# Rotating q and k heads on VectorE alone, scan steps in three operations, and some weight remainders made earlier

## The reference

```python
xn = rmsnorm(x, norm_mix)
u, q, k, v, qi, ki, wi, gl = split(xn @ w_in)
q = rope(rmsnorm(q, q_norm), pos)          # 8 heads of 128
k = rope(rmsnorm(k, k_norm), pos)          # 4 heads of 128
# rope: x1, x2 = halves of a head
#       concatenate([x1*cos - x2*sin, x2*cos + x1*sin])
y_att = attend(q, k, v, qi, ki, wi, pos)   # indexer picks the top keys
# S5: h[t] = a*h[t-1] + (b u)[t], complex, 64 groups x 64 states
y_ssm, h_re, h_im = s5_scan(u, h0, a, b, c, d)
y_ssm = gelu(y_ssm); y_ssm *= sigmoid(y_ssm @ w_glu)
x = x + (gate0 * (y_ssm @ w_br0) + gate1 * (y_att @ w_br1)) @ w_out
x = x + (silu(hn @ w_gate) * (hn @ w_up)) @ w_down   # hn = rmsnorm(x)
```

## Time and profile before

| what | before |
|---|---|
| median of three runs | 3066.21 us |
| profiled execution, its own time | 3065.53 us |
| its span, first to last instruction | 3063.7 us |
| busy: PE, DVE, ACT, POOL | 3006.6, 1956.3, 1240.4, 253.4 us |
| granted TensorE clock, mean over the span | 0.998 |

### The profile page before, as it was taken

One profiled execution on the slowest core, in us unless ns is written; L12 is line 12 of the kernel. 1 busy time (PEld: TensorE's weight loads), 2 busy tenths in 40 slices (PEclk: granted clock), 3 DMA queues, 4 the chain that ended last, 5 costly groups with the idle time before them and its releaser, 6 DMA issues. The chain is left out here.

```text
span 3063.7 us, 58940 instructions
## 1 busy us (share of the span) xinstructions
PE 3006.6 (98%) x23528; PEld 2860.5 (93%) x23528; DVE 1956.3 (64%) x3397; ACT 1240.4 (40%) x1735; POOL 253.4 (8%) x239
## 2 busy tenths in 40 slices
PE   7999999999999999999999999999999999999999
PEld 7988878999999999999989888789999999999999
DVE  7559868577656545565575697785776555456553
ACT  4443333544554333434334422335435453333432
POOL 4320000400000000000043200004000000000000
PEclk9999999999999999999999999999999999999999
DMA  6447434745555655556555573347455556555564
GB/s 249 163 153 196 144 125 137 246 168 177 198 182 181 200 170 178 179 184 206 186 188 167 156 196 127 126 147 244 167 175 199 185 178 201 170 178 182 183 208 134
DMA packets 150194, 546.47 MB, mean 178 GB/s; under 512 B 19825, under 2 KB 25073, under 8 KB 149521
## 3 DMA queue, kind: packets, MB, share of 16 engines
q1 hardware_dynamic: 137296, 507.40, 49.3%
q0 software_dynamic: 12096, 35.67, 4.6%
q10 hardware_dynamic: 640, 1.16, 0.1%
HBM read 536.95 MB, written 7.21 MB: 178 GB/s over the span
## 5 line engine op out<-in xcount | busy, mean ns | idle before, releaser
L1795 DVE TENSOR_TENSOR w_ffn_low<-ring_ffn,w_ffn_high 128x1024 fp32r<-128x1024 f32 (+1 forms) x480 | 638.7, 1331 | 456.9 <-ACT w_ffn_high L1289 456.8
L1289 ACT ACTIVATE w_ffn_high<-ring_ffn 128x1024 fp32r<-128x1024 f32 (+1 forms) x480 | 548.0, 1142 | 641.7 <-PE main L1016 641.5
L1014 PE MATMUL main<-x_ffn_high,w_ffn_high 128*128 128x264 f32 x2816 | 792.5, 281 | 0.0
L1016 PE MATMUL main<-x_ffn_high,w_ffn_low 128*128 128x264 f32 x2816 | 792.1, 281 | 0.0
L1015 PE MATMUL main<-x_ffn_low,w_ffn_high 128*128 128x264 f32 x2816 | 792.1, 281 | 0.0
L1014 PEld LDWEIGHTS main<-x_ffn_high,w_ffn_high 128*128 128x128 f32 x2816 | 527.1, 187 | 0.1
L1015 PEld LDWEIGHTS main<-x_ffn_low,w_ffn_high 128*128 128x128 f32 x2816 | 527.1, 187 | 0.1
L1016 PEld LDWEIGHTS main<-x_ffn_high,w_ffn_low 128*128 128x128 f32 x2816 | 527.1, 187 | 0.0
L1014 PE MATMUL main<-hidden_high,w_ffn_high 128*128 128x264 f32 x1408 | 396.1, 281 | 0.0
L1015 PE MATMUL main<-hidden_low,w_ffn_high 128*128 128x264 f32 x1408 | 396.1, 281 | 0.0
L1016 PE MATMUL main<-hidden_high,w_ffn_low 128*128 128x264 f32 x1408 | 396.1, 281 | 0.0
(11 more groups left out here) (378 smaller groups left out, 4804.0 us busy)
## 6 DMA issues: line engine op xcount, KB each, us to landing
ring_ffn<-in_w_up SPq DMA_DIRECT2D x352, 512.0 KB, 3.3
ring<-in_w_in SPq DMA_DIRECT2D x260, 512.0 KB
ring_ffn<-in_w_down SPq DMA_DIRECT2D x128, 704.0 KB, 4.1
ring<-in_w_br SPq DMA_DIRECT2D x64, 512.0 KB
ring<-in_w_out SPq DMA_DIRECT2D x64, 512.0 KB
w_low<-in_w_in POOLq DMA_DIRECT2D x20, 512.0 KB, 7.0
ring<-in_w_glu SPq DMA_DIRECT2D x16, 512.0 KB
out_x<-x SPq DMA_DIRECT2D x8, 528.0 KB, 5.9
```

The source lines that it names most:

```text
L1014: mm(out, wfh[:, slot, w], high[:, kk, :], start=kk == 0, stop=False)
L1016: m = mm(out, wfl[:, slot, w], high[:, kk, :], start=False, stop=kk == chunks * kts - 1)
L1289: af(wfh[:, s, 0:cols], ring_ffn[:, s, 0:cols], ACT.Copy).then_inc(high_ready, 1)
L1795: tt(wfl[:, s, 0:cols], ring_ffn[:, s, 0:cols], wfh[:, s, 0:cols].bitcast(F32), ALU.subtract).then_inc(low_ready, 1)
```

## The change

Five things change.

1. **Heads are rotated by VectorE alone.** The 12 products with `rot128` and their waits go. VectorE makes the crossed part itself: rows 64 to 127 of the head, times -1 and sin, go to rows 0 to 63 of a buffer, and rows 0 to 63 times sin to rows 64 to 127; then head times cos, and the sum. These 12 x 4 instructions now stand right behind `skip(0)`, beside the second state input, with the lows of units 102 to 105 after every second head. TensorE's pieces of units 106 and 107 become two whole units.
2. **A scan step takes three operations.** One product of 1024 elements makes both parts, with factors from a table that holds, for each tile and each of re and im, the factor of the same part and (negated for im to re) that of the crossed part; then an add of 512 and a crossed add of 512, which reads re and im in the opposite order. Each waits for the one before. The last 15 steps are the same three operations, no longer with two pairs of buffers.
3. **ScalarE makes the tables** (`coefficients`): 8 copies per scan, four of 256 elements and four of 48. For the first scan they stand between the copy of the score and the first state input's copies; for the second behind the copies of v. The scans wait for them.
4. **Lows are made earlier** in the discretization: 13 with 12, 14 and 15 instead of 13 and 14, then 16 before the far powers, 17 and 18 behind them.
5. A semaphore is renamed (`bbt_copied` is now `s5_copied`) and also counts the tables.

```diff
@@ TensorE, after the v transposes
-                    for t in range(12):
-                        pe.wait_ge(qnormed, t + 1)
-                        if t >= 2:
-                            pe.wait_ge(qrot_used, t - 1)
-                        mm(side[t % 2][:, 0:T], rot128, proj[:, K + t, :], start=True, stop=True).then_inc(qrot_ready, 1)
-                        if t % 3 == 1:
-                            w_in_piece(53, t // 3 * 4, 4)
+                    w_in_blocks(53, 1)
@@ ScalarE
+                    def coefficients(half):
+                        tiles = slice(HALF * half, HALF * half + HALF)
+                        for near in (True, False):
+                            table = step_coef[half] if near else far_coef[:]
+                            for kind in range(2):
+                                power = apow[:, kind, :, tiles] if near else far_pow[:, :, kind, tiles]
+                                for c in range(2):
+                                    af(table[:, :, kind, c:ST:2], power, ACT.Copy, scale=-1.0 if kind and c else 1.0).then_inc(s5_copied, 1)
...
+                    act.wait_ge(cneg, 1)
+                    coefficients(0)
                     act.wait_ge(pi_done, 2)
                     bu(0)
...
                         af(vnat[:, b, :], side[2 + b][:, :], ACT.Copy).then_inc(v_copied, 1)
+                    act.wait_ge(units, 106)
+                    coefficients(1)
                     evac_gates(50, 4)
@@ VectorE, discretization
-                    lows_to(12)
+                    lows_to(13)
...
                         if n == 8:
-                            lows_to(14)
+                            lows_to(15)
+                    lows_to(16)
...
-                    lows_to(16)
+                    lows_to(18)
                     dve.wait_ge(c_in, 16)
@@ VectorE, scan
-                            m1, ins = products(pw1, prev, pr, n)
-                            st.mark(ins)
-                            m2, ins = products(pw2, prev, pi, n)
-                            st.link(ins)
-                            st.link(tt(cur, cur, m1, ALU.add))
-                            st.mark(tt(cur[:, :, 0, :], cur[:, :, 0, :], m2[:, :, 1, :], ALU.subtract))
-                            st.link(tt(cur[:, :, 1, :], cur[:, :, 1, :], m2[:, :, 0, :], ALU.add))
+                            m = pw[:, 0:ST * 2 * n].rearrange("p (k m n) -> p k m n", k=2, n=n)
+                            was = prev.rearrange("p s c n -> p (s c) n").unsqueeze(1).to_broadcast([P, 2, ST, n])
+                            st.link(tt(m, was, coef.unsqueeze(3).to_broadcast([P, 2, ST, n]), ALU.mult))
+                            own, crossed = (m[:, kind].rearrange("p (s c) n -> p s c n", c=2) for kind in range(2))
+                            st.link(tt(cur, cur, own, ALU.add))
+                            st.link(tt(cur, cur, crossed[:, :, ::-1, :], ALU.add))
...
                             if j < CH - 1:
-                                m1, ins = products(buf1, last, apow[:, 0, j, tiles], NC - 1)
...
+                                fma(hh[:, :, :, NC * j + 1:NC * j + NC], last, near[:, j], NC - 1)
@@ VectorE, rotation
-                    lows_to(105)
+                    lows_to(101)
+                    dve.wait_ge(qnormed, NHK)
                     for t in range(12):
-                        dve.wait_ge(qrot_ready, t + 1)
+                        tile, buf = proj[:, K + t, :], th[:, t % 2, :]
                         if t >= 2:
                             dve.wait_ge(qroped, t - 1)
-                        rope(proj[:, K + t, :], side[t % 2][:, 0:T], cosq, sinq, th[:, t % 2, :], qrot_used, qroped)
+                        st.mark(stt(buf[0:HD // 2], tile[HD // 2:HD], -1.0, sinq[HD // 2:HD], ALU.mult, ALU.mult))
+                        st.link(tt(buf[HD // 2:HD], tile[0:HD // 2], sinq[0:HD // 2], ALU.mult))
+                        st.link(tt(tile, tile, cosq, ALU.mult))
+                        tt(tile, tile, buf, ALU.add).then_inc(qroped, 1)
+                        if t % 2:
+                            lows_to(min(102 + t // 2, 105))
```

More of the change, by code:

```diff
@@ L142, in build @@
         far = sb("far", [P, 6 * ST])
+        far_coef = sb("far_coef", [P, 3, 2, ST])
         qb = sb("qb", [P, 4, 32])
@@ L279, in build @@
         ktr = cc[:].rearrange("p a b c -> p (a b c)").rearrange("p (b n) -> p b n", b=2)
+        step_coef = [a.rearrange("p (j k m) -> p j k m", j=CH, k=2) for a in (
+            vnat[:].rearrange("p b n -> p (b n)"), bbt[:, 0].rearrange("p f s -> p (f s)"))]
         powers = apow[:].rearrange("p a b c -> p (a b c)")
@@ L312, in build @@
         rows_out = tmp[:, 384:512]
-        pw1, pw2 = tmp[:, 0:512], tmp[:, 512:1024]
+        pw = tmp[:, 0:1024]
         one_hot = rs[:, 1, 0:2 * NHK]
@@ L663, in _ @@
                         if g >= 2:
-                            pe.wait_ge(bbt_copied, g - 1)
+                            pe.wait_ge(s5_copied, g - 1)
                         for j in range(4):
@@ L682, in _ @@
                     pe.wait_ge(proj_copied, 10)
-                    pe.wait_ge(bbt_copied, 3)
+                    pe.wait_ge(s5_copied, 3)
                     for b in range(2):
@@ L689, in _ @@
                     pe.wait_ge(qb_ready, 1)
-                    pe.wait_ge(bbt_copied, 4)
+                    pe.wait_ge(s5_copied, 4)
                     pe.wait_ge(irot_used, 9)
@@ L1573, in scan, with fma @@
                         tiles = slice(HALF * half, HALF * half + HALF)
[L1576 to L1583, removed]
-                            m1, ins = products(pw1, prev, pr, n)
-                            st.mark(ins)
-                            m2, ins = products(pw2, prev, pi, n)
-                            st.link(ins)
-                            st.link(tt(cur, cur, m1, ALU.add))
-                            st.mark(tt(cur[:, :, 0, :], cur[:, :, 0, :], m2[:, :, 1, :], ALU.subtract))
-                            st.link(tt(cur[:, :, 1, :], cur[:, :, 1, :], m2[:, :, 0, :], ALU.add))
-                        a1r, a1i = apow[:, 0, 0, tiles], apow[:, 1, 0, tiles]
+                        dve.wait_ge(s5_copied, 4 + 8 * (half + 1))
+                        def fma(cur, prev, coef, n):
+                            m = pw[:, 0:ST * 2 * n].rearrange("p (k m n) -> p k m n", k=2, n=n)
[4 more added lines that the diff above has]
+                            st.link(tt(cur, cur, crossed[:, :, ::-1, :], ALU.add))
+                        near = step_coef[half]
                         turns = 0
@@ L1607, in scan @@
                         for k in range(4):
                             back, ends = 1 << k, SEQ - NC
-                            pr, pi = (apow[:, c, CH - 1, tiles] if k == 0 else far_pow[:, k - 1, c, tiles] for c in range(2))
                             turn()
-                            fma(hh[:, :, :, ends + back:SEQ], hh[:, :, :, ends:SEQ - back], pr, pi, NC - back)
+                            fma(hh[:, :, :, ends + back:SEQ], hh[:, :, :, ends:SEQ - back],
+                                near[:, CH - 1] if k == 0 else far_coef[:, k - 1], NC - back)
@@ L1613, in scan @@
                         last = hh[:, :, :, SEQ - NC:SEQ - 1]
-                        made = {}
                         for j in range(CH):
                             turn()
-                            buf1, buf2 = pairs[j % 2]
                             if j < CH - 1:
-                                m1, ins = products(buf1, last, apow[:, 0, j, tiles], NC - 1)
-                                made[j] = [m1, st.mark(ins)]
-                            if j >= 1:
-                                cur, (m, n1, w, n2) = hh[:, :, :, NC * (j - 1) + 1:NC * j], made[j - 1]
-                                st.after(n2)
-                                added = st.mark(tt(cur, cur, m, ALU.add))
-                            if j < CH - 1:
-                                if j >= 2:
-                                    st.after(done)
-                                m2, ins = products(buf2, last, apow[:, 1, j, tiles], NC - 1)
-                                made[j] += [m2, st.mark(ins)]
-                            if j >= 1:
-                                st.after(added)
-                                st.mark(tt(cur[:, :, 0, :], cur[:, :, 0, :], w[:, :, 1, :], ALU.subtract))
-                                done = st.mark(tt(cur[:, :, 1, :], cur[:, :, 1, :], w[:, :, 0, :], ALU.add))
```

12 lines of the change are left out of this document (5 added, 7 removed).

## The result

| | before | after |
|---|---|---|
| median of the runs | 3068.84 us (4 runs, 3065.42 to 3075.17) | 3043.06 us (4 runs, 3039.68 to 3045.59) |
| ratio, 95% interval | | 0.9913 [0.9892, 0.9934] |
| span of the profiled execution | 3063.7 us | 3039.8 us |
| busy: PE, DVE, ACT | 3006.6, 1956.3, 1240.4 us | 2994.0, 1965.2, 1247.8 us |

A forecast was written before the change was run, and what follows sets the result against it. TensorE was taken to bound the kernel, with products in a row and few waits. Per layer 7.1 + 1.2 + 2.7 + 1.9 - 1.4 = 11.5 us, twice 23.0, gave 3043 us; range 3032 to 3059.

The forecast's parts named there:

- Rotations: TensorE from the v transposes to the first logits: 16.15 us become about 8.95, so 7.1 us less per layer.
- The cover of 8 us: VectorE's rotated heads are done about 1943, needed from 1950.6 on; gone only at 2.3 us per head.
- The step: A scan step on VectorE takes 2.71 us instead of 2.85; each of the last 15 takes 2.57 instead of 2.33.
- First scan: Beside the bisection: 2.0 us back in the first part, 0.8 lost at the end; 1.2 us less per layer.
- Attention: Beside the second scan: shorter rounds and VectorE entering about 1.1 us ahead cut softmax waits by 2.7 us per layer.
- Low parts: TensorE's waits for lows 13 and 15 go, as these are made earlier: 1.9 us less per layer, bounds 0.5 and 2.4.
- Tables: ScalarE's first eight copies delay the state input's copies, costing 1.4 us per layer; the second eight cost nothing.
- The clock: TensorE's granted clock falls to 1.2 GHz around the picks in layer 1; it can give or take 3 us.
- D: Rival: rotations' gain kept, other waits don't shrink, tables cost 2.6 us; 6 us per layer, 3053 us; 15 in 100.
- A: Rival: links between VectorE instructions are free, last scan steps take about 2.2 us; 3.6 us more gain, 3040; 8 in 100.
- B: Rival: the scan step stays at 2.85 us, last steps 2.71; gain of 2.8 us per layer, 3060; 12 in 100.
- C: Rival: the scan's crossed add pays for stepping backward; at double time 68 us lost in all, 3134; 7 in 100.

The follow-up runs named there:

- e1: The kernel before with only the change's rotations on VectorE; scan and low parts as before, no tables: 3051.06 us, ratio 0.9933 to before.
- e7: The changed kernel with each rotation's two half-height instructions reading the rows they write, so heads aren't rotated properly: 3043.43 us in one run.
- e6: The changed kernel with the crossed add reading re and im in their order, so the scan adds the wrong part: 3042.81 us in one run.
- e5: The changed kernel with each scan's last 15 steps as four instructions of 480, not three linked ones: 3040.69 us, ratio 0.9907 to before.
- e2: The kernel before with the change's rotations and earlier low parts; scan as before, no tables: 3043.13 us, ratio 0.9914 to before.
- e3: The changed kernel with the product of 1024 as two of 512 and the crossed add as two half adds: 3063.04 us, ratio 0.9977 to before.

## Why the prediction was right

The time was forecast at 3043 us and came out at 3043.06. That close is luck: runs of one kernel spread over 4 to 12 us, and the median of before that it was counted from was itself 2.6 us under that of four runs. The gain is 25.8 us by the medians, 23.9 by the spans and 24.4 less the clock, for 23.0 forecast. What isn't luck is that the terms came out one by one.

- **Rotations, 7.1.** 7.3 and 7.2 in the traces, 7.1 in e1. What was wrong is "0.35 + 0.46 + 0.46 + 0.35" for a head: all are 0.46, as e7 explains. The cover of 8 us was the reason why that couldn't matter, and 5.8 us of it were left.
- **The step, 2.71 and 2.57.** Measured to 0.02 us. It rested on two neighbours, a broadcast product of 1024 and linked adds; the operand without a neighbour, backward through re and im, turned out free (e6).
- **First scan, 1.2.** 1.9 gained in the turns, 0.8 given back at the pick. The turn of the pace, VectorE being the slower one with linked last steps, was in the walk, and e5 shows that it is this: with last steps of 2.28 us the wait goes.
- **Attention, 2.7.** 2.5 on balance. The late wait of 0.66 us, 1.0 by the lead, isn't named in the prediction; e5 shows that the linked last steps make it. The 1.1 us of VectorE's head start are in e1 alone (1.0).
- **Low parts, 1.9.** 2.4 by the leads on average, 2.1 by the waits of e1 and e2. I had counted the two waits and not the little beside them.
- **Tables, 1.4 lost.** 1.5 in either layer. Eight copies took 1.77 us, 0.31 per copy of 256 elements and 0.13 per one of 48, beside the 0.3 and 0.1 that I took. With these my own sum is 1.2 + 0.4 - 0.35 = 1.25 and not 1.4, so the closeness of this term is luck by 0.15 us.
- **Not foreseen:** the transfer of unit 87, 1.5 us in all, which by e1 comes and goes between traces of the same program, at least in layer 0.
- **The clock.** Equal in both profiles, 10.2 us at the lower rate. I had put it in the range with 3 us; with 6.8 to 20.5 us in the others it makes up to 7 us between two runs, more than most of the edits. I had also put it at the picks, and it falls behind the products that spread the heads' norms.
- **Range.** Its lower end doesn't follow from its terms: 3043 less 6 less 3 is 3034, not 3032. D's 6 us per layer lead to 3054, not 3053. Neither changes a verdict.

The rivals: A by e5 (a link costs 0.12 us), B and C by the rows of the step, and e3 shows that B would have left 5 us of gain by the medians and 8 less the clock, where 6 were worked out. D, waits that don't shrink, is refuted by the waits themselves.

## What to carry to other kernels

Where two engines go in step, a small piece of either is multiplied by the number of steps in which that engine is the slower one; walking both engines through the turns with durations from the trace gave it to 0.2 us here (1.2 and 2.7 for 1.1 and 2.5). Busy time wouldn't have: VectorE's rose by 8.9 us. Compare two kernels with the clock's share taken off, run by run: the medians here couldn't tell the scan's part from nothing. When an engine's work is fused into fewer instructions, look whether they now all depend on the one ahead: three linked instructions took 2.57 us, four that needn't wait 2.28. And a preparation that moves to an idle engine should stand where that engine really waits, since this one, though small, stood just ahead of the copies that TensorE was about to need.

## What the runs showed of the hardware

- On VectorE an fp32 instruction that waits for the one ahead follows 0.11 to 0.12 us later than one that doesn't (0.69 against 0.57 at 480 elements, 0.46 against 0.35 at 264).
- An fp32 product of 1024 with both factors broadcast takes 1.20 to 1.23 us, one with a single factor 1.22, and an add that reads a dimension backward takes what a forward one takes (0.69 for 512).
- An instruction whose rows start elsewhere than those of the instruction ahead (0 and 64 here) follows as if it waited for it: 0.46 instead of 0.35, and 1.24 instead of 1.13 after a low part.
- TensorE's time at the lower clock differs between profiles of nearly the same kernel by up to 13.7 us, about half of which goes into the time. In layer 1 of the changed kernel the clock falls twice, each time within 1 us of the end of 2.9 us of products with 12 of 128 rows.
